# Prompt rows moved from the query stage into the merge, and the first routing group searched score block by score block

## The reference, cut to what matters

```python
def merge_branches(h, branches, w_branch, w_gate, b_gate, w_out):
    gates = jax.nn.sigmoid(h @ w_gate + b_gate)
    merged = 0
    for i, y in enumerate(branches):
        merged = merged + gates[..., i * D_MODEL:(i + 1) * D_MODEL] * (y @ w_branch[i])
    return merged @ w_out
...
        qry = (hc @ w_query).reshape(-1, PEER_HEADS, 2, PEER_DK // 2)
        s = jnp.einsum('thpk,hpnk->thpn', qry, sub_keys, preferred_element_type=F32)
        s1, i1 = lax.top_k(s[:, :, 0], PEER_TOPK)
        s2, i2 = lax.top_k(s[:, :, 1], PEER_TOPK)
        cand = (s1[..., :, None] + s2[..., None, :]).reshape(-1, PEER_HEADS, PEER_TOPK * PEER_TOPK)
        sc, ci = lax.top_k(cand, PEER_TOPK)
...
        act = jax.nn.gelu(jnp.einsum('thkd,td->thk', u_tab[e], hc, preferred_element_type=F32), approximate=False)
        return jnp.einsum('thk,thkd->td', (g * act).astype(hc.dtype), v_tab[e])
```

## Time and profile before

| | us |
|---|---|
| median of 3 runs | 5171.96 |
| lowest, highest | 5168.32, 5173.55 |
| the profiled execution | 5164.73 |
| its span | 5162.9 |
| busy: TensorE, VectorE | 4427.5, 3387.4 |
| busy: ScalarE, GpSimd | 1951.4, 1663.2 |

### The profile page before, as it was taken

One profiled execution on the slowest core, in us unless ns is written; L12 is line 12 of the kernel. 1 busy time (PEld: TensorE's weight loads), 2 busy tenths in 40 slices (PEclk: granted clock), 3 DMA queues, 4 the chain that ended last, 5 costly groups with the idle time before them and its releaser, 6 DMA issues.

```text
span 5162.9 us, 46892 instructions
## 1 busy us (share of the span) xinstructions
PE 4427.5 (86%) x14388; PEld 2284.0 (44%) x14388; DVE 3387.4 (66%) x7266; ACT 1951.4 (38%) x5074; POOL 1663.2 (32%) x1600
## 2 busy tenths in 40 slices
PE   7889878998899888888888887999888987777777
PEld 4674355434645333344544434644464632222222
DVE  4249754777787677775444885777778767676544
ACT  1210443443233434565533034534323343333333
POOL 3003021323243453443332322132224344344332
PEclk8899989999999999999999998999999999999999
DMA  7752416999799999999999133189979999999998
GB/s 286 267 176 74 173 65 239 347 351 362 286 420 420 415 420 420 412 394 417 406 419 412 57 130 130 62 324 349 354 279 420 415 416 422 421 421 419 422 421 351
DMA packets 277115, 1677.27 MB, mean 325 GB/s; under 512 B 31808, under 2 KB 31856, under 8 KB 112384
## 3 DMA queue, kind: packets, MB, share of 16 engines
q0 software_dynamic: 190896, 1365.43, 65.5%
q1 hardware_dynamic: 82944, 302.03, 15.9%
q10 hardware_dynamic: 3024, 6.82, 0.3%
HBM read 1667.33 MB, written 6.82 MB: 324 GB/s over the span
## 4 chain that ended last, share of the span: by engine, by line
DMA 42%; PE 29%; DVE 17%; ACT 6%; issue 6%; POOL 0%; SPq 0%; DVEq 0%; ACTq 0%; POOLq 0%
DMA arena<-experts,bsb 26%; DMA arena<-experts,peidx 13%; PE ps L2217 13%; PE ps L1804 5%; DVE arena L1495 4%; DVE arena L1707 3%; DVE arena L1406 2%; PE ps L1912 2%; DMA wring<-w 2%; PE ps L2069 2%; PE ps L2091 2%; PE ps L1780 1%; ACT T L1069 1%; ACT L1065 1%; ACT bsb L1066 1%
## 5 line engine op out<-in xcount | busy, mean ns | idle before, releaser
L2217 PE MATMUL ps<-arena,T 128*128 128x512 f32 x4096 | 1970.8, 615 | 442.4 <-ACT T L1069 436.5
L1707 DVE CUSTOM_DVE_ANT_0 arena<-arena,h_sb 128x1024 f32<-128x1024 f32 x1024 | 1250.4, 1225 | 868.8 <-DMA arena<-experts,bsb 857.5
L680 POOL DMA_INDIRECT arena<-experts,bsb x1024 | 1093.0, 1067 | 1745.6 <-PE ps L2217 1590.0
L2217 PEld LDWEIGHTS ps<-arena,T 128*128 128x128 f32 x4096 | 727.3, 192 | 1568.8 <-ACT T L1069 934.6
L1065 ACT ACTIVATE bsb<-T 128x1 f32<-128x1 f32 x1024 | 206.0, 201 | 1312.6 <-DVE T L1707 1309.6
L1804 PE MATMUL ps<-h_sb,wring 128*128 128x256 f32 (+2 forms) x2304 | 517.4, 381 | 35.5 <-DVE h_sb L1446 13.7
L2128 PE MATMUL ps<-h_sb,wring 128*128 128x512 f32 x1024 | 457.4, 600 | 33.7 <-DVE arena L1632 31.5
L1804 PEld LDWEIGHTS ps<-h_sb,wring 128*128 128x128 f32 x2304 | 379.9, 196 | 184.6 <-issue 152.6
L663 POOL DMA_INDIRECT arena<-experts,peidx x224 | 251.5, 1123 | 617.3 <-DVE arena L1406 581.5
L1396 DVE CUSTOM_DVE_ANT_0 arena<-arena,h_sb 128x1024 f32<-128x1024 f32 x256 | 312.6, 1222 | 186.8 <-DMA arena<-experts,peidx 185.5
L1069 ACT ACTIVATE T<-ident,bsb 128x128 f32<-128x128 f32 x1024 | 410.9, 401 | 33.5
(11 more groups left out here) (326 smaller groups left out, 4539.1 us busy)
## 6 DMA issues: line engine op xcount, KB each, us to landing
wring<-w SPq DMA_DIRECT2D x576, 512.0 KB
arena<-experts,bsb POOLq DMA_INDIRECT x1024
bsb<-bias POOLq DMA_DIRECT2D x16, 512.0 KB, 3.8
arena<-subk POOLq DMA_DIRECT2D x4, 1024.0 KB, 10.6
arena<-experts,peidx POOLq DMA_INDIRECT x256, 8.1
arena<-v_scratch POOLq DMA_DIRECT2D x64, 64.0 KB, 2.0
x_sb<-xT POOLq DMA_DIRECT2D x1, 2048.0 KB, 14.3
v_scratch<-arena ACTq DMA_DIRECT2D x8, 256.0 KB, 2.0
```

Source lines behind the costliest of these rows:

```text
L680: gp.indirect_dma_start(rows[:, n % NS, :], None, experts, bass.IndirectOffsetOnAxis(ap=eidx[:, t % 2, i:i + 1], axis=0)).then_inc(row_in[ ...
L1707: v.tensor_tensor_reduce(e, e, htok(t), 1.0, 0.0, ALU.mult, ALU.add, dots[:, t % 2, i:i + 1]).then_inc(dot, 1)
L2217: mm = pe.matmul(ps[:, 6 + half, :], diag[:, n % ND, :], rows[:, n % NS, D + half * 512:D + (half + 1) * 512], start=(i == 0), stop=(i == ...
```

## The change

1. The table of prompt rows: a merge step n below 30 has (13(n+1)//4 - 13n//4) rows, so 3, 3, 3, 4 and again, 97 in all; step 30 has none; step 31 has seven, and those stand behind the last sum and its signal. The 8 output steps keep one each. The query stage has none.
2. Tile 0's first routing group starts with the query stage. Behind the copy of each of the score blocks 0 to 7, VectorE does all five operations on that block, each waiting for the one before. The rest of the routing still takes 10 yields per step from step 8 on. The other groups are searched as before.

```diff
 def prompt_rows_at(stage, n):
 
     if stage == "merge":
-        return range(EARLY + 3 * n, EARLY + 3 * n + 3)
-    if stage == "out":
-        return range(112 + n, 113 + n)
-    return range(120 + n, 121 + n) if n < 8 else ()
+        return range(EARLY + 13 * n // 4, EARLY + 13 * (n + 1) // 4) if n < 30 else range(EARLY + 97, EARLY + 104) if n == 31 else ()
+    return range(EARLY + 104 + n, EARLY + 105 + n) if stage == "out" else ()
...
-            def route(l, r, sc, eidx_out, gate_out, idx_sem, top_sem, gate_free):
+            def route(l, r, sc, eidx_out, gate_out, idx_sem, top_sem, gate_free, by_unit=False):
...
+                for i in range(2 * GH) if by_unit else ():
+                    own.link(v.max(top[:, i, 0:8], sc[:, i, :]))
+                    own.link(v.max_index(topi[:, i, 0:8], top[:, i, 0:8], sc[:, i, :]))
+                    own.link(v.match_replace(sc[:, i, :], top[:, i, 0:8], sc[:, i, :], LOWEST))
+                    own.link(v.max(top[:, i, 8:16], sc[:, i, :]))
                     own.tick(v.max_index(topi[:, i, 8:16], top[:, i, 8:16], sc[:, i, :]))
                     yield
+                if not by_unit:
...
-                    if n == 8:
+                    if n == 0:
                         prompt_add(l, PAIRS - 1)
-                        for k in range(4, 8):
-                            wait_freed(v, u(f"s{k}"))
-                        first = latent_route(0, 0)
-                    if first:
-                        for _ in range(10):
-                            next(first, None)
+                        first = latent_route(0, 0, True)
+                    if 1 <= n <= 8:
+                        wait_freed(v, u(f"s{n - 1}"))
+                        next(first)
+                    for _ in range(10 if n >= 8 else 0):
+                        next(first, None)
```

More of the change, by code:

```diff
@@ L1134, in route @@
                 topf4 = topf.rearrange("p (h s) k -> p h s k", s=2)
[L1135 to L1151, removed]
+                for i in range(2 * GH) if by_unit else ():
[3 more added lines that the diff above has]
+                    own.link(v.max(top[:, i, 8:16], sc[:, i, :]))
                     own.tick(v.max_index(topi[:, i, 8:16], top[:, i, 8:16], sc[:, i, :]))
                     yield
+                if not by_unit:
+                    for i in range(2 * GH):
+                        own.tick(v.max(top[:, i, 0:8], sc[:, i, :]))
+                        yield
+                    own.wait()
+                    for i in range(2 * GH):
+                        own.tick(v.max_index(topi[:, i, 0:8], top[:, i, 0:8], sc[:, i, :]))
+                        yield
+                    own.wait()
+                    for i in range(2 * GH):
+                        own.tick(v.match_replace(sc[:, i, :], top[:, i, 0:8], sc[:, i, :], LOWEST))
+                        yield
+                    own.wait()
+                    for i in range(2 * GH):
+                        own.tick(v.max(top[:, i, 8:16], sc[:, i, :]))
+                        yield
+                    own.wait()
+                    for i in range(2 * GH):
+                        own.tick(v.max_index(topi[:, i, 8:16], top[:, i, 8:16], sc[:, i, :]))
+                        yield
                 own.wait()
@@ L1678, in second_half, with latent_route @@
                         yield
-                def latent_route(t, g):
+                def latent_route(t, g, by_unit=False):
                     return route(l, lroute, scores[:, t, 8 * g:8 * g + 8, :], eidx[:, t % 2, GP * g:GP * (g + 1)], gate[:, t % 2, GP * g:GP * (g + 1)],
-                                 idx_ready, top_ready, lambda: need(v, diag_ok, (l * NL + t - 1) * PAIRS))
+                                 idx_ready, top_ready, lambda: need(v, diag_ok, (l * NL + t - 1) * PAIRS), by_unit)
                 def latent_soften(t, g):
```

## The result

| | before | after |
|---|---|---|
| median of the runs, us | 5171.91 | 5206.41 |
| lowest, highest | 5159.67, 5182.80 | 5194.01, 5218.14 |
| profiled execution, its span | 5164.73, 5162.9 | 5203.20, 5201.4 |

The ratio is 1.0068, 95% interval 1.0046 to 1.0090: slower, by 34.5 us. The forecast was 5204, slower.

What follows compares the result with a forecast made beforehand. Merge rows are paid by the late engine, VectorE; from the first latent gather the DMA bounds. Per layer 24.8 - 9.8 + 11.9 - 11.1 = +15.8 us; 5171.96 + 31.6 = 5204, range 5186 to 5224.

Steps and rivals of the forecast that it cites:

- Part 2: Merge: four rows instead of three in seven steps, each 2.34 us of work plus 1.2 of waiting, +24.8 us per layer.
- Rival (a): Fourth rows and the seven find data ready, only VectorE's work counts: +4.9 us per layer, 5182; chance 0.17.
- Part 3: End of merge: no row in step 30, -9.8 us to the last sum; seven rows behind it, +11.9.
- +11.9: Behind the last sum: seven rows instead of three before the first output addition, 9.4 us of work plus 2.5 of waiting.
- the 1.4 us that I had as the upper end: Behind the last sum: most that each of the next four rows would wait; 6.3 us in all, 2.5 taken.
- Part 1: Query stage: block-by-block search gives indices 13.7 us earlier, of which 11.1 us per layer reach the DMA.
- the deduction of 2.6 us for weight chunks: Start of latent gathers: two weight chunks of 1.3 us each go beside the gathers, taken off the 13.7 us.
- Rival (b): Routing gain arrives only as VectorE's earlier start, 6.2 us: +20.7 us per layer, 5213; chance 0.13.
- Rival (c): Merge: TensorE at 10.5 us is the true pace and its lead absorbs the rows: -9.0 us per layer, 5154; chance 0.12.
- The query stage: Between merge and gathers: TensorE's pace, 3.90 us a block, so it gives nothing back for its eight rows.
- The sum: Per layer: +26.9 us until the second norm, -11.1 us behind it, +15.8 us.
- The first latent gather: After the routing: the first latent gather in the new profile comes 13 us later than before.

Runs made afterwards that it cites:

- e3: Kernel before with merge step 30's three rows moved behind the last sum (six there); run twice: ratio to before 0.9976, then 1.0001.
- v3: Before with the first group's search cut into single operations spread over query steps, and step 30's three rows behind the last sum: 5154.89 us against 5172.94, ratio 0.9962.
- e2: After with the old search, so only the prompt rows' new places differ from before: 5224.53 us against before's 5176.86, ratio 1.0105.
- v2: After with the last yields of the first routing spread as 8, 8, 7, 4, 3: 5201.69 us against before's 5176.86, ratio 1.0059.
- e4: Before with the 112 later prompt gathers fetching 4 KB a token in place of 8: 5091.46 us against before's 5175.25, ratio 0.9823.
- e5: After with the 112 later prompt gathers fetching 4 KB a token in place of 8: 5113.66 us against before's 5175.25, ratio 0.9861.

## Why the prediction was right

*Part 2, the four-row steps, was right in size and reason.* Forecast +24.8 us, measured +25.1. The waits that were to be added are there: a fourth row waits 1.2 us in the mean, as taken, and the steps are at 14.9 and 11.2 us (forecast 15 and 11.2). Rival (a), no extra waiting, falls: seven rows cost 25.1, not 16.4. The pair's waits for rows alone would not show it, 41.2 to 49.1 us in layer 0 but only 46.8 to 48.4 in layer 1, since step 30's rows are gone as well. With step 30 empty in both, the waits are 42.0 us per layer without the four-row steps (e3 twice, v3) and 50.8 with them (after, e2, v2), and 8.7 is what 25.1 has over 16.4.

*Part 3, the end of the merge.* Forecast -9.8 up to the last sum, measured -9.6 (24.1 us in 10 stretches, 14.5 in 12). For what follows I had said +11.9; the pooled out stages with seven rows take 50.6 against 39.5, +11.1, and this trace pair has +10.3. That this came out near is luck. The parts of the term were both off, and cancelled (layer 0): behind the last sum the first addition comes 15.1 us later than before (22.4 against 7.3), since the seven rows waited 5.5 us and not 2.5 (four times the 1.4 us that I had as the upper end make about that, and not the 6.3 that I wrote); but the rest of the stage, which was to stay as it was, is 4.7 us shorter (27.0 against 31.7), since the eight rows in it waited 4.4 us in all, where before they waited 9.1. Why they wait less there was not tried. TensorE's wait for the last sum, 1.8, is under 3 as forecast; its new one, 12.7, is a little over the 6 to 12.

*Part 1, the search, was right in the indices and wrong in what was taken off.* Indices 13.7 us earlier: 34.9 to 21.2. Of this I let 11.1 reach the gathers; 9.6 did. The mis-sized term is the deduction of 2.6 us for weight chunks: in v2 all that is lost, chunks included, is 0.9 (13.0 to 12.1), so chunks cost no more than that, and in after 4.1 is lost, most of it by an edge that I had not looked at. The last ten yields before the indices, 9 us of work, stand in front of two score copies; TensorE waits 2.56 us for them, and POOL's eighth gather for TensorE's transposes. Rival (b), that the gain arrives only as VectorE's earlier start, falls: behind block 7's copy the first dot came only 1.9 us earlier, and the 121st 9.6. In after's layer 0 seven gathers had been issued by 1394.90, 7 us ahead of that dot.

*Rival (c)* falls: in layer 0 VectorE's product waits for the gate 30 times and never for TensorE, and even between e4 and e5, where the data come sooner, most of the rows' time is paid. TensorE's step is 10.30 us, not 10.5 (the ends of its blocks overlap).

*The query stage*, forecast 0, grew by 0.4 us. *The sum*: +14.5 for the merge (364.3 pooled over 349.8; forecast 15.0), +11.1, +0.4, -9.6, makes +16.4 per layer against 15.8; the one trace pair has 15.7. The medians differ by 34.5 us, and their interval goes from 24 to 47, so that 5204 came within 3 us of 5206.41 is closer than either the forecast or the measurement could promise.

*The first latent gather* was forecast 13 us later than before. POOL issues it at 1384.62, before at 1364.37: 20.3 later, of which 6.1 lie ahead of the merge, so 14.2. The first dot is another matter: 1401.94 against 1369.87, 32 us later. Its data were there; VectorE sat idle 5.4 us ahead of it for the gate's exponential, which ScalarE makes behind the transposes, and TensorE's stop had made those late.

## What to carry to other kernels

A row of work moved from a stage where another engine is late into one where its own engine is late costs its own time, and more if its data are not there yet: here 3.6 us for 2.34 us of work, with four buffers that the old spacing of three rows a step kept just ahead. It pays to look first for room where the work already is: the search fitted between the copies without moving a row, once its instructions were spread to the length of a step. When a fill is spread over steps, size each group by the copy it stands in front of: 9 us of it here stopped TensorE, and through it the queue of gathers that it was to start sooner.

## What the runs showed of the hardware that was not expected

The bytes of the prompt rows cost the merge nearly all that its waits for them showed: with half of them (e4) 41.2 us of waits went, and the merge is 34 us shorter. The window that had TensorE busy for 45.71 us at a DMA share of 0.91 has it busy throughout, at 0.70; and the prompt rows' median time from issue to landing is 5.6 us over both layers, where before it was 8.1.

```profile
1150.00:1200.00 50.00, 50.00 (x118) 22.13 (x117) 39.85 (x53) 23.23 (x43) 19.52 (x15) 1.00 0.70 233
```

```profile
arena<-experts,peidx POOLq DMA_INDIRECT x256, 5.6
```

TensorE's slow stretch moved with its stop. Before, behind the wait of 11.67 us for the last sum, the granted clock was 0.50 (1.2 GHz) for the first 5 us, and the 48 matmuls of the first three output blocks took 13.25 us. After, behind 1.81 us, it was 1.00 (2.4 GHz) and they took 10.63; the clock was 0.50 behind the 12.66 us instead, where 16 matmuls took 5.17 us in place of 3.62. In e3b, behind a wait of 3.60 us, it was 0.50 again, and the 48 took 13.26. It cost nothing in before and after, since none of the output additions waited for TensorE. Windows and blocks, the first window of before, the second of e3b, the rest of after:

```profile
1249.45:1254.45 5.00, 5.00 (x12) 4.01 (x13) 4.91 (x7) 1.00 (x4) 1.68 (x1) 0.50 0.75 283
```

```profile
1240.42:1245.42 5.00, 5.00 (x12) 4.01 (x13) 4.77 (x6) 0.99 (x4) 1.68 (x1) 0.50 0.70 285
```

```profile
1272.30:1282.30 10.00, 10.00 (x47) 8.83 (x48) 7.39 (x10) 1.49 (x6) 4.29 (x3) 1.00 0.92 364
1296.52:1299.00 2.48, 2.48 (x7) 2.02 (x6) 1.62 (x3) 0.86 (x3) 0.94 (x1) 0.50 0.96 330
```

```profile
1198.03 10.13 PE L2134 MATMUL ps<-h_sb,wring 128*128 128x512 f32 x16 [3.12 <-DVE arena L1638]
...
1272.22 10.63 PE L1810 MATMUL ps<-arena,wring 128*128 128x256 f32 x48 [1.81 <-DVEq L1644]
1295.51 1.22 PE L2147 MATMUL ps<-arena,ones 128*128 128x256 f32 x2 [12.66 <-ACT arena L1008]
1296.52 5.17 PE L1810 MATMUL ps<-arena,wring 128*128 128x256 f32 x16
```

The same happens inside after's merge, where TensorE stops behind four-row steps: behind the wait of 3.12 us the gate block took 10.13 us in place of 7.03, at a granted clock of 0.50 (1198.03 to 1203.00), and the window from 1150 to 1200 has 0.91 where before has 1.00. So TensorE is later behind its stops than its 10.30 us a step would make it; VectorE's products in layer 0 still did not wait for it.

Stages that no edit touched varied: layer 0's first product is at 898.6 to 910.2 us in twelve traces and at 928.7 in one, and from layer 0's 121st dot to layer 1's first product the eleven traces with whole prompt rows have 1656.9 to 1668.4 us. The merge of identical code varied by 8.7 us (346.0 to 354.7), where the query and gather stages of identical code repeat within 1 us. A sum by stages is worth more than one span against another.
